# Weaving a gated-delta pass into a state-space scan, regrouping a quarter combination, and a second f buffer in a one-core transformer kernel

## The reference, cut to what matters

```
ssd:  a scan over chunks:   state = state * decay + B^T xc;   y = C state * exp(a) + (C B^T * L) xc
gdn:  per chunk of the sequence
      sol   = triangular_solve(strict(beta k k^T * decay), [beta v, beta k exp(g)])   # u, w
      v_new = u - w state;   o = (q exp(g)) state + (q k^T * decay) v_new
      state = state * exp(g_last) + (k exp(g_last - g))^T v_new
x  = x + rmsnorm(concat(att, ssd, gdn) @ w_out) * gain
h  = rmsnorm(x)
f  = silu(h @ ffn_w_gate) * (h @ ffn_w_up);   x = x + rmsnorm(f @ ffn_w_down) * gain
```

## Time and profile before

| | us |
|---|---|
| median of three executions | 2412.46 |
| the profiled execution | 2409.74 |
| its span | 2407.9 |
| TensorE busy in the span | 2177.4 |
| VectorE / ACT / POOL busy | 1191.2 / 854.3 / 844.4 |
| mean granted TensorE clock | 0.961 of full |

### The profile page before, as it was taken

The page is one execution under the profiler, slowest core; times in us unless marked ns, Lnnn a source line. Parts: engine busy times, 40 slices in busy tenths (PEclk is TensorE's granted clock), DMA queues, the critical chain, the costliest instruction groups (busy, mean ns, idle before and its releaser), DMA issues.

```text
span 2407.9 us, 29829 instructions
## 1 busy us (share of the span) xinstructions
PE 2177.4 (90%) x11123; PEld 1833.4 (76%) x11123; DVE 1191.2 (49%) x1693; ACT 854.3 (35%) x1754; POOL 844.4 (35%) x575
## 2 busy tenths in 40 slices
PE   6999988768994999999999986789999999999896
PEld 5888877657784788888888875668888888888775
DVE  4444415855415835555555546678994235111223
ACT  4332135544335542222222216237774112000134
POOL 2222322322222666666666641220000323333221
PEclk9999999879997999999999998999999999999998
DMA  4111311020212111111111132210001111111121
GB/s 149 44 44 44 88 38 25 14 75 1 96 45 79 35 43 52 52 53 53 51 54 53 51 111 93 82 29 1 1 1 31 44 53 44 44 53 44 53 96 70
DMA packets 176479, 125.99 MB, mean 52 GB/s; under 512 B 25316, under 2 KB 161232, under 8 KB 176208
## 3 DMA queue, kind: packets, MB, share of 16 engines
q1 hardware_dynamic: 160864, 91.77, 13.2%
q10 hardware_dynamic: 15472, 32.31, 3.7%
HBM read 106.77 MB, written 17.30 MB: 52 GB/s over the span
## 4 chain that ended last, share of the span: by engine, by line
PE 69%; DVE 18%; ACT 7%; issue 3%; POOL 2%; SPq 1%; DMA 0%; ACTq 0%; DVEq 0%; POOLq 0%
PE gemm L965 15%; PE gemm L967 15%; PE gemm L966 15%; PE gemm L984 5%; PE gemm L986 4%; PE gemm L985 4%; DVE PT L1682 3%; DVE a2m L2116 3%; PE side L1016 2%; PE side L994 2%; PE side L1144 1%; POOL wsum L843 1%; POOL w_lo L856 1%; DVE x L2078 1%; ACT sqp L1285 1%
## 5 line engine op out<-in xcount | busy, mean ns | idle before, releaser
L965 PE MATMUL gemm<-h_hi,w_hi 128*128 128x512 f32 x1328 | 524.2, 395 | 8.2 <-DVE h_lo L2148 8.2
L967 PE MATMUL gemm<-h_hi,w_lo 128*128 128x512 f32 x1328 | 518.8, 391 | 0.0
L966 PE MATMUL gemm<-h_lo,w_hi 128*128 128x512 f32 x1328 | 518.4, 390 | 0.0
L860 POOL TENSOR_SCALAR w_hi<-w_raw 128x1024 fp32r<-128x1024 f32 x113 | 129.8, 1149 | 1056.6 <-issue 985.7
L965 PEld LDWEIGHTS gemm<-h_hi,w_hi 128*128 128x128 f32 x1328 | 250.4, 189 | 61.7 <-issue 8.1
L967 PEld LDWEIGHTS gemm<-h_hi,w_lo 128*128 128x128 f32 x1328 | 250.1, 188 | 53.0
L966 PEld LDWEIGHTS gemm<-h_lo,w_hi 128*128 128x128 f32 x1328 | 250.5, 189 | 49.9
L863 POOL TENSOR_TENSOR w_lo<-w_raw,w_hi 128x1024 fp32r<-128x1024 f32 x113 | 280.3, 2480 | 9.4
L1712 DVE TENSOR_TENSOR accT<-accT,gemm 128x1024 f32<-128x1024 f32 x80 | 97.7, 1221 | 119.8 <-PE gemm L967 119.6
L856 POOL TENSOR_TENSOR w_lo<-wsum,w_hi 128x512 fp32r<-128x512 f32 x100 | 137.3, 1373 | 25.4 <-ACT w_hi L1366 19.1
L965 PE MATMUL gemm<-f_hi,w_hi 128*128 128x512 f32 x352 | 138.4, 393 | 6.8 <-DVE f_lo L1760 6.8
(11 more groups left out here) (397 smaller groups left out, 4084.2 us busy)
## 6 DMA issues: line engine op xcount, KB each, us to landing
w_raw<-in_w_in SPq DMA_DIRECT2D x60, 512.0 KB, 3.8
w_raw<-in_ffn_w_gate SPq DMA_DIRECT2D x22, 512.0 KB, 3.8
w_raw<-in_ffn_w_up SPq DMA_DIRECT2D x22, 512.0 KB, 4.1
w_raw<-in_ffn_w_down SPq DMA_DIRECT2D x22, 512.0 KB, 3.8
w_raw<-in_w_out SPq DMA_DIRECT2D x16, 512.0 KB, 4.2
x_spill<-x ACTq DMA_DIRECT2D x4, 2048.0 KB, 7.1
xin<-in_x SPq DMA_DIRECT2D x8, 512.0 KB, 6.4
x<-in_x ACTq DMA_DIRECT2D x1, 4096.0 KB, 15.2
```

Of the source, the lines that this page charges most:

```text
L860: gp.tensor_scalar(hi[:], raw[key % 4][:], 1.0, 0.0, ALU.mult, ALU.add).then_inc(pool_hi, 1)
L965: mm(o, hi[:, k, m], act[0][:, k, t], start=k == 0, stop=False)
L966: mm(o, hi[:, k, m], act[1][:, k, t], start=False, stop=False)
L967: last = mm(o, lo[:, k, m], act[0][:, k, t], start=False, stop=k == kt - 1)
```

## The change

Three edits. (1) The `inv` steps go eight to a chunk from chunk 1 on, so they end in chunk 4. Chunk 7 of the scan is interleaved with `gx` 0 to 2, `ly` and `lx` of chunks 0 and 1, and `uw` 0. The delta loop starts at chunk 0, with `gx` of chunk c+3 first in pass c. The second `sn` moves from the end of the scan to the end of delta pass 1. (2) Combination 1 of the activations is added after the whole residual is done; its low part is computed on VectorE, and combination 0 is added by POOL after the second halves of the first two `gate` units and after the low part of combination 1. (3) The last pair's f goes to a buffer of its own, `f_end`; the `down` units of pair 9 move from between the last pair's `gate` and `up` products to behind them. `gbc2` moves to another address.

```diff
@@ weight_units
-        if p > 0:
+        if 0 < p < NF // 2 - 1:
             down(p - 1)
         up(2 * p)
         up(2 * p + 1)
+    down(NF // 2 - 2)
     down(NF // 2 - 1)
@@ schedule, the scan
-        s += [("yd", c), ("ap", c), ("st", c)] + [("sg", c + 1), ("as", c + 1)] * more + [("ao", c)]
-        s += [("yo", c + 1)] * more + [("sa", c + 2)] * (c + 2 < NT) + [("inv", n) for n in islice(steps, 6 * (c > 0))]
-        s += [("sn", c // 4)] * (c % 4 == 3)
+        if more:
+            s += [("yd", c), ("ap", c), ("st", c), ("sg", c + 1), ("as", c + 1), ("ao", c), ("yo", c + 1)]
+            s += [("sa", c + 2)] * (c + 2 < NT) + [("inv", n) for n in islice(steps, 8 * (c > 0))] + [("sn", 0)] * (c == 3)
+        else:
+            s += [("gi", 0), ("gx", 0), ("yd", c), ("ap", c), ("ly", (0, 5)), ("gx", 1), ("st", c), ("lx", (0, 5)), ("ao", c)]
+            s += [("ly", (0, 6)), ("ly", (1, 5)), ("lx", (0, 6)), ("lx", (1, 5)), ("uw", 0), ("gx", 2)]
@@ schedule, the delta pass
-    s.append(("gi", 0))
-    for c in range(-3, NT):
-        s += at("ly", c + 1, 6) + at("r1", c) + at("ly", c + 2, 5) + at("lx", c + 1, 6) + at("r2", c)
-        s += at("lx", c + 2, 5) + at("uw", c + 1) + at("gx", c + 3)
-        s += [("gn", n) for n in range(len(NORMED) - 1) if NORMED[n] == c]
+    for c in range(NT):
+        s += at("gx", c + 3) + at("ly", c + 1, 6) + at("r1", c) + at("ly", c + 2, 5) + at("lx", c + 1, 6) + at("r2", c)
+        s += at("lx", c + 2, 5) + at("uw", c + 1)
+        s += [("gn", n) for n in range(len(NORMED) - 1) if NORMED[n] == c] + [("sn", 1)] * (c == 1)
@@ schedule, gate and up
-          [("resid", (0, 0)), ("norm", (1, 0)), ("load", 6), ("csum", 1), ("comb", 1), ("resid", (0, 1)), ("load", 7)],
-          [("norm", (1, 1)), ("csum", 0), ("comb", 0)])
-    s += [("csum", 2), ("comb", 2), ("csum", 4), ("csum", 3), ("unit", by["up", 0]), ("unit", by["up", 1]), ("comb", 3), ("comb", 4)]
+          [("resid", (0, 0)), ("norm", (1, 0)), ("load", 6), ("resid", (0, 1)), ("load", 7)],
+          [("csum", 1), ("norm", (1, 1)), ("comb", 1)])
+    s += [("csum", 0), ("comb", 0), ("csum", 2), ("comb", 2), ("csum", 4), ("csum", 3), ("unit", by["up", 0]), ("unit", by["up", 1]), ("comb", 3), ("comb", 4)]
     for p in range(1, NF // 2):
         s += [("mul", (by["gate", 2 * p], i)) for i in range(7)]
-        run([("down", (p - 1, j)) for j in range(8)])
+        if p + 1 < NF // 2:
+            run([("down", (p - 1, j)) for j in range(8)])
         s += [("mul", (by["up", 2 * p], i)) for i in range(7)]
     s.append(("load", 8))
+    run([("down", (NF // 2 - 2, j)) for j in range(8)])
@@ buffers
+        f_end = [sbuf("f_end_hi", [2, T], 108, F32R), sbuf("f_end_lo", [2, T], 116, F32R)]
-        gbc2 = sbuf("gbc2", [D], 108)
+        gbc2 = sbuf("gbc2", [D], 124)
@@ POOL, csum
+                        if j == 1:
+                            pool.wait_ge(N["resid_done"], 8)
+                        elif j == 0:
+                            pool.wait_ge(N["comb_lo"], k + 1)
                         step(gp.tensor_tensor(dst, x, y, op), "comb_sum")
-                        if j == 1 and k > 0:
-                            step(comb_low(pool, 1, k - 1), "comb_lo1")
-                    if j == 1:
-                        step(comb_low(pool, 1, 3), "comb_lo1")
@@ VectorE, comb
-                elif kind == "comb" and j in (0, 3, 4):
+                elif kind == "comb" and j != 2:
```

More of the change, by code:

```diff
@@ L548, in build_program @@
             "ssd_rs", "gdn_rs", "pool_step", "sq_part", "rs_ready",
-            "hf_ready", "comb_sum", "comb_add", "comb_hi", "comb_lo", "comb_lo1", "w_sum", "w_quarter_hi", "t_copied", "sg_ready", "f_made")}
+            "hf_ready", "comb_sum", "comb_add", "comb_hi", "comb_lo", "w_sum", "w_quarter_hi", "t_copied", "sg_ready", "f_made")}
         z_out = [sem(f"z_out{i}") for i in range(2)]
@@ L633, in mul_part, with f_tiles @@
             return m, slice(512 * t, 512 * t + 512)
+        def f_tiles(p):
+            return f_end if p == NF // 2 - 1 else fT
         def pairs_before(n):
@@ L947, in unit @@
                     banks_free(pe, n)
-                act = {"down": fT, "ya": atT, "yb": gmT}.get(kd[0], hT)
+                act = f_tiles(kd[1][0]) if kd[0] == "down" else {"ya": atT, "yb": gmT}.get(kd[0], hT)
                 if kd[0] == "down":
@@ L978, in mul @@
                     if j[0] == unit_of["gate", 2] and MUL[j[1]] not in (1, 4):
[L979 to L982, removed]
+                        pe.wait_ge(N["comb_lo"], {3: 1, 0: 5, 2: 9, 6: 13, 5: 17}[MUL[j[1]]] + k)
                     b = mul_operand(j[1], k)
@@ L1332, in unit @@
                 elif kind == "down" and j[0] == 0:
-                    act.wait_ge(N["comb_lo"], 16)
+                    act.wait_ge(N["comb_lo"], 20)
                     gemm_product(act, n)
@@ L1382, in final @@
                         act.wait_ge(N["f_made"], count)
-                        step(af(fT[0][:, m, t], sg[m][:, t], ACT.Copy), "f_hi")
+                        step(af(f_tiles(units[n]["kind"][1] // 2)[0][:, m, t], sg[m][:, t], ACT.Copy), "f_hi")
                 if i in (0, 1, 3):
@@ L1388, in mul @@
                     else:
-                        act.wait_ge(N["comb_lo"], 8)
+                        act.wait_ge(N["comb_lo"], 12)
                     gemm_product(act, j)
@@ L1759, in f_low @@
                         dve.wait_ge(N["f_hi"], 2 + before + (2, 4, 5, 6).index(i) + 1)
-                        step(v.tensor_tensor(fT[1][:, m, t], sg[m][:, t], fT[0][:, m, t], ALU.subtract), "f_lo")
+                        f = f_tiles(units[n]["kind"][1] // 2)
+                        step(v.tensor_tensor(f[1][:, m, t], sg[m][:, t], f[0][:, m, t], ALU.subtract), "f_lo")
                 if i == 0:
```

## The result

The changed kernel takes 2388.43 us (median of four executions, 2386.28 to 2389.03), the kernel before 2413.64 in the same series (2412.39 to 2414.89). The ratio is 0.9894 with a 95% interval of 0.9877 to 0.9911: faster by 25 us. Later series had the kernel before at 2407.5 to 2410.0 (44 executions in four series), and the changed kernel, run again in one of them, at 2387.59 with a ratio of 0.9908. So the gain is nearer 22 us, and some 3 of the 25 come from the first runs of before, which were slower than the later ones. The profiled spans are 2407.9 and 2386.5, 21.4 apart.

What follows compares the result with a forecast made beforehand. TensorE bounds the kernel (69% of the chain), so edits pay only where it stands still. -17.9 + 3.1 - 4.4 = -19.2 on 2409.74 gives 2390.5, with 2.7 for the median 2393.3; range 2386 to 2400, 8 in 10 2383 to 2405.

Steps and rivals of the forecast that it cites:

- (a): Scan, chunks 1 to 4: added inverse steps cost their length, +5.3 us (bounds 3 and 7).
- (b): Scan to delta pass: transfers hide behind chunks 5 and 6, data 5 us early, pass 0 starts at 526: -10.5 us.
- (c): Delta passes 1 to 5: gx one pass ahead removes the 2.24 us wait for ACT's X/XT: -11.2 us.
- (d): Delta passes: sn 1 and gn 0 there delay VectorE and ACT, +3.8 us (bounds +1 and +7).
- part 2: Combination at the head: norm 4.5 us earlier, but VectorE's added low parts make up 1 late: +3.1 us.
- part 3: End of the last feature pair: TensorE's 6.78 us wait goes, a 2.4 us bank wait comes: -4.4 us.
- Part 1: Woven start and delta passes: (b), (c) and (d) together, -17.9 us.
- the locked pieces: Combination at the head: by the lock rule VectorE's pieces beside POOL's adds take 2.35 us, not 1.66; part 2 near +8.6.
- stiffer weave: Rival, 0.18: start at the lower clock, in-order ACT holds ap 7 behind gx 0; whole change -7 us, 2405.
- Nothing measurable: Rival, 0.07: inverses land after ACT is ready, or the edit orders work without making it earlier; 2408.
- VectorE did not keep up: Rival, 0.10, that VectorE keeps up at the head: part 2 at -4.5, whole change -28 us, 2384.5.
- the slower case: Rival, 0.05: clock stays at the lower level in the delta passes, each 6.9 us more; all six +22, 2435.

Runs made afterwards that it cites:

- the run with fewer steps: The changed kernel with 6, 6, 6, 6 and 7 inverse steps in chunks 1 to 5, not 8, 8, 8, 7: 2383.60 against 2387.59 us.
- the last two kernels: Changed kernel with combination 0's sums between splits, sn 1 behind pass 5, steps 5, 6, 6, 6, 6, 2: 2378.91; then sums ahead, in own buffers: 2376.39.
- the weave alone: The kernel before with only the first of the three edits: 17.6 us faster (14.7 to 20.7).
- the f buffer alone: The kernel before with only the third edit, the second f buffer for the last pair: 6.5 us faster (3.4 to 9.9).

## Why the prediction was right, and where it was off

The sign, the place and the order of all three parts were right. The forecast of 2393.3 is 4.9 above the measured median. By the spans it is off by 2.2 (19.2 forecast, 21.4 measured); the rest came from adding 2.7 us from the profiled execution of before to the median of three runs, where the median of 44 later executions is 2409.7, level with the profiled one.

That the sum came so close is in part luck. In the profile, (a) and (b) brought 5.3 us less than forecast; (c) and (d), part 2 and part 3 together brought 3.6 more, the end of the last delta pass 0.9, and 2.8 came from stages that the change doesn't touch.

**(a) Inverse steps: mis-sized.** Forecast +5.3, measured +8 (8.0 to 8.2 in three traces; 10.5 in the profile after). The prediction charged the steps their length and named no neighbour. Its own sum for lengths was fair. The term that was missing is some 0.7 us for each step instruction that meets a POOL product. There are four more of them than before in the three traces with +8, which is 2.9 us, and 5.3 and 2.9 are 8.2; the profile after has five.

**(b) The hand-over: right in its mechanism, late by (a).** The margin was forecast at 5 us. The reissue ended at 506.66, and in the run with fewer steps, where ACT waits for the data, it starts 1.8 us behind the reissue; so the data lay there 4.9 us before ACT's X. The chain from X to pass 0 took 18.0 us, 19 forecast. Pass 0 came 5.2 us earlier and not 10.5, and in this trace (a) alone is 5.2 above its forecast (2.5 of it go with the later return of the clock).

**(c) The passes: right, a little small.** Five passes without the wait save 12.4 us (10.83 to 8.34 each, as the undisturbed passes show), 11.2 forecast, since TensorE's own 8.59 also shrank to 8.34. Putting `gx` back costs 11.5: shown.

**(d) `sn` 1 and `gn` 0 in the passes:** +3.8 forecast, +3.4 by the passes (9.34 on average over five against 8.34, and 11.16 against 10.83 before). One near 12 was forecast; pass 3 took 11.49. The size is right and the account behind it is not. Of the 3.2 us for `sn` 1 it put 0.6 on VectorE and the rest on ACT's load while it also spreads X; `sn` 1 cost 3.9, and 2.3 of them stayed in a place where ACT has no X to spread. `gn` 0 was to cost 0.6 more than before, since its cover was gone; it cost 1.6 before, and 1.2 with `sn` 1 out of its way. The two misses cancel.

Part 1 in all: -17.9 forecast, -15.2 in the profile, -17.6 (14.7 to 20.7 faster) in the run by itself.

**Part 2:** +3.1 forecast, +2.0 in the profile, +1.7 by itself. `up` 1 is multiplied 2.15 us later against the residual, 3.1 forecast; VectorE's stand (6.64) was not in the sum as such, but its late arrival was. The norm came 4.5 us earlier, as forecast.

The 8.6 us of the locked pieces came from taking 1.06 and 1.29 us as the times alone. The 1.06 is a mean over three instructions of 1.00, 0.69 and 1.41 us, the last of them beside a weight split. In the profile after, VectorE's piece when POOL is quiet, POOL's sums while VectorE stands still, and then both beside each other:

```profile
796.97 0.69 DVE L630 TENSOR_TENSOR cmb<-m,cmb 128x512 fp32r<-128x512 f32 x1
...
747.87 3.97 POOL L890 TENSOR_TENSOR m<-hfull 128x512 f32<-128x512 f32 x3 [37.95 <-DVE x L2086]
...
790.17 3.37 DVE L1815 TENSOR_TENSOR m<-hfull 128x512 f32<-128x512 f32 x2
...
787.97 6.72 POOL L890 TENSOR_TENSOR hfull<-hfull 128x512 f32<-128x512 f32 x4
```

One behind the other, 0.69 and 1.29 are 1.98; beside each other the engines move at 1.70 a piece. So they take turns for most of an instruction, though 0.3 us less than for its whole length. That is near the rule of the Trainium skill ("SBUF — State Buffer", "Who interferes with whom"), in which VectorE with two SBUF inputs and a GpSimd instruction that reads SBUF, as here, block each other while one of them runs, and far from the 2.35 a piece that the prediction drew from it; the step instructions above, which end 0.2 us behind POOL's, agree with it as nearly.

**Part 3:** -4.4 forecast, -5.3 in the profile, -6.5 by itself. The bank wait is 1.70, 2.4 forecast. The prediction also had no term for the clock: in the 5 us behind the 6.78 us wait it was 0.61, behind the 1.70 us wait 1.00. Which of the two makes the difference was not separated.

**The rivals.** The stiffer weave fell: the start took 18.0 us at a mean granted clock of 0.81, with TensorE busy 15.57 of them, and the weave by itself brought 17.6 us and not 9. "Nothing measurable" fell with the data landing 4.9 us early. VectorE did not keep up in this change; it does with sums in buffers of their own. The clock was 0.86 in pass 0, as before, and 1.00 in passes 1 to 5, so the slower case did not come.

## What to carry to other kernels

An instruction added to a full engine costs its length plus what it meets: look up what the engine that slows it in the trace does at that very time. Where an engine stands for a result, ask first whether the producer waits on a reused buffer; for combination 0 a few idle kilobytes were worth more than either of the other places tried for its sums. A mean over merged instructions is no time alone. And before a profiled execution is set against a median of three, look at how far executions of one kernel scatter: here 2404 to 2416.

## What the runs showed of the hardware that was not expected

**The clock comes back at one of two times.** Around `sn` 0 TensorE is busy about half of 12 us (5.9 us in the profile after, 5.4 in the changed kernel run again) and its granted clock falls to the lower level, 0.50 and 0.57 on average. What follows, in the same place of the same kernel, the first from the profile after and the second from the changed kernel run again:

```profile
477.00:485.00 8.00, 8.00 (x48) 7.33 (x48) 5.60 (x15) 4.70 (x16) 0.00 (x0) 0.71 0.00 0
```

```profile
479.20:487.20 8.00, 6.92 (x55) 6.18 (x54) 7.28 (x22) 5.61 (x18) 0.00 (x0) 1.00 0.00 0
```

In the first the clock is at the lower level until some 4 us behind the attention maximum, in the second it is back at the maximum. With 1.00 in these 8 us the chunk takes 14.8 to 15.4 us from maximum to maximum (the kernel before and four of the experiments). With the later return, 0.70 to 0.73, it takes 17.4 to 18.3 (the profile after and six experiments), and 15.5 in the last two kernels, where VectorE has only 3.7 us of inverse steps in that chunk (4.5 in the profile after, 6.2 in the run with 6, 6, 6, 6 and 7); whether that is the whole reason was not tried. For the same kernel the difference is 2.6 us in this chunk, and no edit made it. What decides the return was not tried.

**Which of two engines is first decides who is stretched.** In the second block VectorE's `rpd` (128x2048) takes 2.29 us alone. Beside POOL's weight split, in the kernel before and in the profile after:

```profile
1559.85 2.65 POOL L863 TENSOR_TENSOR w_lo<-w_raw,w_hi 128x1024 fp32r<-128x1024 f32 x1
...
1560.34 4.31 DVE L1918 TENSOR_TENSOR rpd<-rp,rp 128x2048 f32<-128x2048 f32 x1
```

```profile
1540.92 3.01 DVE L1926 TENSOR_TENSOR rpd<-rp,rp 128x2048 f32<-128x2048 f32 x1
...
1541.88 4.27 POOL L873 TENSOR_TENSOR w_lo<-w_raw,w_hi 128x1024 fp32r<-128x1024 f32 x1
```

Where POOL began first, `rpd` took 4.31; where `rpd` began first, POOL's split took 4.27. TensorE waits 3.4 us less for `rpd` in the profile after. But the same kernel run again has POOL first and `rpd` at 4.32, as have the weave alone and the f buffer alone. So the 1.5 us that this stage seemed to gain are no gain of the change. With 0.4 us in the attention behind it, at a clock of 0.98 and not 0.96, they are 1.9 of the 2.8 us that the three parts leave over; the other 0.9 were not followed.
